# A table of relative biases fetched in two parts behind different weight units, and a small row fetched later

## The chip, the core and the metric

The kernel runs on one core of one Trainium2 chip. Its time is in device microseconds (us), from the start of one execution to its end, and the figure compared is the median of several executions. Inside the core five engines run side by side, each with an instruction stream of its own: TensorE (PE in the profile), VectorE (DVE), ScalarE (ACT), GpSimd (POOL) and SyncE (SP). They meet only at semaphores. SP, ACT and POOL also issue DMA transfers; each has a queue of its own (q1, q10 and q0 in the profile), and the queues share the core's 16 DMA engines.

## What is computed

Three transformer-like layers over one sequence of 256 tokens with 1024 channels, all in float32. Layer 0 attends with a relative position bias for each of eight heads, layer 1 is a differential attention with a scalar made from `diff_lambda`, and layer 2 is a convolution module. The change touches the inputs of the first two. Cut to what matters:

```python
def t5_bucket(rel): ...                       # distance -> one of 32 buckets
# layer 0: attention, for every head
rel_own = q_pos[:, None] - k_pos_own[None, :]
bias_own = jnp.moveaxis(rel_table[t5_bucket(rel_own)], -1, 0)
s_own = einsum('bhqd,bhkd->bhqk', qb, k_own) + bias_own[None]
s_own = jnp.where(rel_own >= 0, s_own, NEG_INF)
p = jax.nn.softmax(...)
# layer 1: differential attention
lam_full = (jnp.exp(jnp.sum(lam32[0] * lam32[1])) - jnp.exp(jnp.sum(lam32[2] * lam32[3]))
            + lambda_init)
a = p[:, :, 0] - lam_full * p[:, :, 1]
```

## The kernel before

The program has six stages, `s` = 0 to 5: attention, gated product, attention, gated product, convolution, gated product. Weights arrive in *units* of 128 x 1024 float32 (512 KB). A unit goes into one of eight slots of `raw`; ACT rounds it into `whi` (L893), DVE writes the rest into `wlo` (L1203), and PE multiplies both with the two parts of the activations (`h_hi`, `h_lo`). Semaphore `ld[u]` says that slot `u` has landed, `hi[u]` and `lo[u]` that it has been split. The helper `prep(u, n)` on ACT and on DVE is one half of this split.

In stage 0 the order is as follows.

- SP first loads 16 quarters of `ada_w` for the modulation vectors (L305), which DVE sums into `acc` (L1225, L1228). Then it loads the units of the first pair of heads in the order of slots 0, 2, 1, 3, 5, 4 (L266): q and k of head 0, q and k of head 1, then the two halves of v. The next units (slot 0, slot 2 and so on for heads 2 and 3) follow as slots come free. A column unit is fetched in rows of 512 bytes.
- ACT issues the small parameters at the start (`params`, L909). The last of them is the lambda row: 256 floats repeated over 128 partitions into `lam_in`, which is a part of `mix` that is first read in stage 2.
- The bias is made in three steps. PE looks up a row of 384 values for each head, DVE adds the causal fill into `relrow` (L1282), and POOL stores it to a small tensor in memory, `rel_small` (L456). Then POOL reads it back skewed, so that partition p starts at element p + 1, into `head_bias` (L461): 128 partitions x 8 heads x 384. It does so in two transfers for all heads (columns 0 to 255, and 256 to 383), after waiting for `ld[3]`, the fourth unit. The two post-norm gain rows, `Ga` and `Gf` (L419), follow on the same queue.
- DVE waits for both bias transfers before the first head. The first DVE instruction that reads them is L1350, which adds the bias to a head's scores. The next ones find the row maximum (L1357, L1360), ACT takes the exponential (L1039), and DVE divides (L1365, L1369).

One attention step (`step`, head n) on ACT is, in this order: copy q (L1021), copy k (L1023), `prep` of two units for a later head (L893, twice), exponential (L1039), `prep` of one unit, copy v (L1048) on even heads, `prep` of one more unit, then q of the next head (L1021). On DVE: bias and maximum, two `prep`, division, more `prep` and some steps of the modulation sums (L1215), which read quarters of `ada_raw`. PE does q and k of a head (L491), the scores (L662, L663), v (L686) on even heads, then q and k of the next head, and only then transposes this head's probabilities (L637), for which it also waits until ACT has copied the next q.

The `lam_in` row is used by `lam_and_gain` at the start of the second attention.

Of the kernel before, what the change touches and what calls it, by code (L numbers as in the profile page):

```python
# [61 lines left out]
def build(nc, x, c, rel_bias, ada_w, ada_b, norm_g, moba_w_qkv, moba_w_o, diff_w_qkv, diff_w_o,  # L62
# [4 lines left out]
    with ExitStack() as ctx:  # L67
# [114 lines left out]
        used = [sem(f"unit_multiplied{u}") for u in range(8)]  # L182
        ada_ld = [sem(f"ada_loaded{k}") for k in range(4)]
        odd_ld = [sem(f"first_odd_loaded{k}") for k in range(4)]
        gemv, first_mm, bias0_loaded = sem("gemv_steps"), sem("first_quarters_multiplied"), sem("first_bias_loaded")
        acc_zero, acc_bias = sem("acc_zero"), [sem(f"acc_bias{n}") for n in range(1, 7)]
        c_loaded, par_loaded, x_loaded = sem("c_loaded"), sem("par_loaded"), sem("x_loaded")
        rel_loaded, rel_mm, rel_row = sem("rel_loaded"), sem("rel_mm"), sem("rel_row")
        rel_stored, bias_loaded = sem("rel_stored"), sem("bias_loaded")
        lam_loaded, lam_seq, lam_exp = sem("lam_loaded"), sem("lam_seq"), sem("lam_exp")  # L190
        b2_loaded, gain_loaded = sem("b2_loaded"), sem("gain_loaded")
        id_zero, consts = sem("id_zero"), sem("consts")
# [208 lines left out]
        def _(pool):  # L401
# [38 lines left out]
            for s in range(LAST + 1):  # L440
                for t in range(TT):
                    pool.wait_ge(ssx_done, 2 * s + t + 1)
                    pool.tensor_tensor(rsx[:, t:t + 1], ssx[:, t:t + 1], mhalf, ALU.pow).then_inc(rsx_done, 1)
                if s in (2, 4):
                    pool.wait_ge(mod_gf, s // 2)
                    pool.wait_ge(hlo, h_parts_before(s + 1))
                    acc_init(s + 2, s // 2, 5 * D, 6 * D)
                    gains(s // 2)
                elif s in (1, 3):
                    pool.wait_ge(mod_ga, s // 2 + 1)  # L450
                    pool.wait_ge(mod_cols, s + 1)
                    pool.wait_ge(hlo, h_parts_before(s + 1))
                    acc_init(s + 2, s // 2 + 1, 0, 5 * D)
                if s == 0:
                    pool.wait_ge(rel_row, 1)
                    pool.dma_start(rel_small, relrow).then_inc(rel_stored, 16)  # L456
                    pool.wait_ge(rel_stored, 16)
                    pool.wait_ge(ld[3], 16)
                    for lo_c, hi_c in ((0, 2 * P), (2 * P, 3 * P)):
                        src = bass.AP(rel_small.tensor, rel_small.offset + 1, [[1, P], [REL, H], [1, hi_c - lo_c]])  # L460
                        pool.dma_start(head_bias[:, :, lo_c:hi_c], src).then_inc(bias_loaded, 16)  # L461
                    gains(0)
                if s == 2:
                    def head_rstd(i):
                        for at in range(2 * TT):
                            t = at % TT
                            pool.wait_ge(oss, i * 4 + at + 1)
                            pool.tensor_tensor(mso[:, t:t + 1], sso[:, t:t + 1], eps2, ALU.add).then_inc(oms, 1)
                            pool.wait_ge(oms, i * 4 + at + 1)
                            pool.tensor_tensor(rso[:, t:t + 1], mso[:, t:t + 1], mhalf, ALU.pow)\  # L470
                                .then_inc(ors, 1)
                    with pool.Fori(0, NI_A) as i:
                        head_rstd(i)
                if s == 4:
                    pool.wait_ge(lms_done, 1)
                    pool.tensor_tensor(ln_rs, ln_ms, mhalf.broadcast_to([P, TT]), ALU.pow).then_inc(lrs_done, 1)
                for t in range(TT):
                    rstd_y(s, t)
# [409 lines left out]
        def _(act):  # L888
# [44 lines left out]
            params(prow[2 * FT:4 * FT, 3, :], rows(f_dw_b_2), par_loaded)  # L933
            params(prow[0:16 * KT, 4, :], rows(a_dw_w_2[0, 0:16]), par_loaded)
            params(prow[0:15 * KT, 5, :], rows(a_dw_w_2[0, 16:CONV]), par_loaded)
            params(lam_in, bass.AP(diff_lambda.tensor, diff_lambda.offset, [[0, P], [1, 256]]), lam_loaded)

            pre_stats(0)
            for t in range(TT):
# [259 lines left out]
        def _(dve):  # L1199
# [120 lines left out]
            def attention(s):  # L1320
# [63 lines left out]
                def first_attention_step(i, j):  # L1384
                    n = i * 2 + j
                    last = n == H - 1

                    def sums(m0, m1):
                        for m in range(m0, m1):
                            gemv_step(0, FIRST + m // KT, m % KT)  # L1390

                    def between():

                        if n:
                            out_lo((n - 1) // 2, 1 - j)
                        if not last:
                            prep(j, i + (nb + 1))
                            prep(2 + j, i + (nb + 1))

                    m0, m1 = 2 * HEAD_QUARTERS[n], 2 * HEAD_QUARTERS[n + 1]  # L1400
                    ahead = m0 + (m1 - m0) // 2 if n > 1 else m0
                    sums(m0, ahead)
                    softmax(n + hb, n, None, between)
                    prep(6 + j, i + nb3)
                    if not last:
                        sums(ahead, m1)
                        prep(4 + j, i + (nb + 1))
# [308 lines left out]
            for s in range(LAST + 1):  # L1716
# [10 lines left out]
                        prep(4 + j, USE[s][2])  # L1727
                if s in (0, 2):
                    if s == 0:
                        dve.wait_ge(bias_loaded, 32)  # L1730
                        gemv_start(2)
                    else:
                        lam_and_gain()
# [51 lines left out]
```

## Time and profile before

| | |
|---|---|
| median of 3 executions | 1019.33 us (1019.18 to 1020.24) |
| the profiled execution's own time | 1019.02 us |
| its span, from the first to the last instruction | 1017.2 us |
| PE busy | 975.5 us (96%) |
| DVE busy | 844.4 us (83%) |
| ACT busy | 543.9 us (53%) |
| moved by DMA | 233.52 MB, mean 230 GB/s |
| mean granted TensorE clock | 0.978 of full |

PE is the engine that is seldom idle; all others have slack on average. Averages hide that stage 0 begins with the transfers at their limit, so the first 60 us have to be read by themselves. In the rows further down, a number in brackets at the end of a row is the idle time of the engine before that row, and behind the arrow stands what ended it.

### The profile page before, as it was taken

Reading aid. Unit: us, or ns where it says so; the run is one execution under the profiler, and the core shown is the slowest. Engines: PE = TensorE matmul, PEld = TensorE weight load, DVE = VectorE, ACT = ScalarE, POOL = GpSimd, SP = SyncE. Lnnn points to the kernel's source line nnn. Section 1 sums busy time; section 2 is a strip of 40 time slices with the busy share of each in tenths; the row PEclk is TensorE's granted clock in tenths of the full one; section 3 lists DMA queues with packets and bytes.
Section 4 is the critical chain, followed back from the end, with each engine's and each line's share of the span. In section 5 each row is a group of like instructions: output and inputs, shape, how many; then the busy total and the mean of one; then the engine's idle time right before and its main releaser. Section 6 shows DMA issues by size and latency. Waiting matters only on the chain.

```text
span 1017.2 us, 19351 instructions
## 1 busy us (share of the span) xinstructions
PE 975.5 (96%) x6742; PEld 892.6 (88%) x6742; DVE 844.4 (83%) x1381; ACT 543.9 (53%) x1016; POOL 57.7 (6%) x99
## 2 busy tenths in 40 slices
PE   5899999999999999998999999999998999999997
PEld 4889988999999888996999999979995889999996
DVE  5869988888888779777898888889998879997775
ACT  2455545454444467555544444459997455555552
POOL 2100002000000012112200000010000000000000
PEclk9999998999999999999999999999998989999999
DMA  9999982999999865661699999974330548966641
GB/s 338 325 333 317 318 272 77 348 340 337 309 312 310 259 187 165 168 196 54 182 347 340 330 311 310 302 232 126 105 103 21 153 125 239 269 186 186 186 124 42
DMA packets 259087, 233.52 MB, mean 230 GB/s; under 512 B 7513, under 2 KB 208986, under 8 KB 259034
## 3 DMA queue, kind: packets, MB, share of 16 engines
q1 hardware_dynamic: 256256, 226.52, 73.2%
q0 software_dynamic: 1504, 4.80, 1.3%
q10 hardware_dynamic: 1274, 1.52, 0.4%
q8 instruction: 30, 0.49, 0.2%
q14 instruction: 23, 0.19, 0.1%
HBM read 231.75 MB, written 1.06 MB: 229 GB/s over the span
## 4 chain that ended last, share of the span: by engine, by line
PE 49%; DVE 8%; issue 4%; ACT 2%; POOL 1%; DVEq 0%; POOLq 0%; ACTq 0%
PE work L491 29%; PE Y L511 14%; DVE mix L1645 3%; PE work L686 2%; ACT whi L893 1%; DVE wlo L1203 1%; DVE xt L1317 1%; DVE acc L1215 1%; PE Y L848 0%; DVE Y L1313 0%; ACT h_hi L964 0%; PE Y L803 0%; POOL small L427 0%; PE work L652 0%; PE work L668 0%
## 5 line engine op out<-in xcount | busy, mean ns | idle before, releaser
L491 PE MATMUL work<-h_hi,whi 128*128 128x256 f32 x1440 | 409.0, 284 | 7.3 <-DVE h_lo L1261 5.9
L1203 DVE TENSOR_TENSOR wlo<-raw,whi 128x1024 fp32r<-128x1024 f32 x286 | 347.1, 1222 | 77.3 <-ACT whi L893 77.0
L491 PE MATMUL work<-h_hi,wlo 128*128 128x256 f32 x1440 | 403.9, 280 | 0.0
L491 PE MATMUL work<-h_lo,whi 128*128 128x256 f32 x1440 | 403.8, 280 | 0.0
L893 ACT ACTIVATE whi<-raw 128x1024 fp32r<-128x1024 f32 x286 | 298.0, 1054 | 150.0 <-PE work L491 44.0
L491 PEld LDWEIGHTS work<-h_hi,whi 128*128 128x128 f32 x1440 | 272.2, 189 | 15.8 <-DVE h_lo L1261 6.8
L491 PEld LDWEIGHTS work<-h_lo,whi 128*128 128x128 f32 x1440 | 272.0, 189 | 3.1
L491 PEld LDWEIGHTS work<-h_hi,wlo 128*128 128x128 f32 x1440 | 272.6, 189 | 0.0
L1215 DVE SCALAR_TENSOR_TENSOR acc<-ada_raw,csil,acc 128x512 f32<-128x512 f32 (+1 forms) x256 | 190.8, 747 | 6.0 <-DMA ada_raw<-in_ada_w 3.4
L511 PE MATMUL Y<-whi,ab_hi 128*128 128x512 f32 x308 | 97.7, 398 | 0.0
L511 PE MATMUL Y<-whi,ab_lo 128*128 128x512 f32 x308 | 96.7, 395 | 0.0
L511 PE MATMUL Y<-wlo,ab_hi 128*128 128x512 f32 x308 | 96.5, 394 | 0.0
L511 PEld LDWEIGHTS Y<-whi,ab_lo 128*128 128x128 f32 x308 | 57.7, 187 | 13.9
L511 PEld LDWEIGHTS Y<-wlo,ab_hi 128*128 128x128 f32 x308 | 57.8, 188 | 13.9
L511 PEld LDWEIGHTS Y<-whi,ab_hi 128*128 128x128 f32 x308 | 52.5, 188 | 7.0
L1645 DVE SCALAR_TENSOR_TENSOR mix<-mix,taps 128x256 f32<-128x256 f32 x128 | 51.4, 477 | 0.0
L1097 ACT ACTIVATE ab_hi<-mix 128x256 fp32r<-128x256 f32 x66 | 27.2, 412 | 39.1 <-DVE mix L1556 20.7
L427 POOL TENSOR_TENSOR small<-small 128x1 f32<-128x1 f32 x12 | 6.6, 554 | 703.2 <-DVE small L1311 703.2
L1089 ACT ACTIVATE mix<-work 128x256 f32<-128x256 f32 x44 | 16.7, 380 | 47.1 <-PE work L491 47.1
L1137 ACT ACTIVATE wlo<-ident,taps 128x128 fp32r<-128x128 f32 x104 | 40.4, 389 | 0.0
L1137 ACT ACTIVATE whi<-ident,taps 128x128 fp32r<-128x128 f32 x104 | 40.4, 389 | 0.0
L1039 ACT ACTIVATE mix<-mix,small 128x128 f32<-128x128 f32 (+1 forms) x48 | 21.4, 447 | 34.5 <-DVE small L1360 34.5
(206 smaller groups left out, 1180.3 us busy)
## 6 DMA issues: line engine op xcount, KB each, us to landing
ada_raw<-in_ada_w SPq DMA_DIRECT2D x88, 512.0 KB, 6.6
raw<-in_ffn_w_in SPq DMA_DIRECT2D x88, 512.0 KB, 7.8
ada_raw<-in_mod_w SPq DMA_DIRECT2D x48, 512.0 KB, 6.6
raw<-in_ffn_w_out SPq DMA_DIRECT2D x44, 512.0 KB, 5.7
raw<-in_f_up_w SPq DMA_DIRECT2D x44, 512.0 KB, 3.9
raw<-in_moba_w_qkv SPq DMA_DIRECT2D x24, 512.0 KB, 8.2
raw<-in_diff_w_qkv SPq DMA_DIRECT2D x24, 512.0 KB, 7.2
raw<-in_a_pw_w SPq DMA_DIRECT2D x24, 512.0 KB, 5.7
```

Source lines behind the costliest of these rows:

```text
L491: mm = pe.matmul(dst, w[:, u, ws], h[:, k, :], start=(k == 0 and m == 0), stop=(k == KT - 1 and m == 2))
L511: mm = pe.matmul(Y[:, 2 * t + f, :], a[:, ts], w[:, u, f * 512:(f + 1) * 512], start=(first and m == 0), stop=False)
L686: mm = pe.matmul(work[:, 1, t * S:(t + 1) * S], h[:, k, ts], w[:, 4:6, ws], start=(k == 0 and m == 0), stop=(k == KT - 1 and m == 2))
L893: act.activation(whi[:, u, :], raw[:, u, :], ACT.Copy).then_inc(hi[u], 1)
L1039: act.activation(pr[:, g, a:b], pr[:, g, a:b], ACT.Exp, bias=mneg[:, m:m + 1], accum_out=msum[:, m:m + 1]).then_inc(ex_done, 1)
L1089: act.activation(gate[:, j, :], work[:, 2 * j, 0:S], ACT.Silu).then_inc(gate_done, 1)
L1097: act.activation(a_hi[:, j, :], act32[:, j, :], ACT.Copy).then_inc(ahi, 1)
L1137: d = act.activation(diag[w][:, m, :], ident[:], ACT.Copy, scale=taps[:, j, 36 + w * NP + m:37 + w * NP + m])
L1203: dve.tensor_tensor(wlo[:, u, :], raw[:, u, :], whi[:, u, :].bitcast(F32), ALU.subtract).then_inc(lo[u], 1)
L1215: dve.scalar_tensor_tensor(at, ada_raw[:, k, q % 2, :], csil[:, ccol:ccol + 1], at, ALU.mult, ALU.add).then_inc(gemv, 1)
L1317: dve.scalar_tensor_tensor(xt[:, t, :], yG, rsy[:, t:t + 1], xt[:, t, :], ALU.mult, ALU.add).then_inc(x_ready, 1)
L1645: v = dve.scalar_tensor_tensor(sums, u[:, m:m + S], w, sums, ALU.mult, ALU.add)
```

## The change

`head_bias` is fetched in four transfers in place of two. The two column parts of head 0 are issued when `ld[0]`, the first unit, has landed; those of heads 1 to 7 when `ld[3]` has landed. There are two semaphores, and DVE waits for head 0's in front of head 0's L1350 and for the others' in front of head 1's. The lambda row is no longer ACT's last parameter but POOL's last transfer of this group, behind the gain rows. The numbers of bytes are the same.

```diff
-        rel_stored, bias_loaded = sem("rel_stored"), sem("bias_loaded")
+        rel_stored, bias_loaded = sem("rel_stored"), (sem("first_bias_loaded"), sem("other_biases_loaded"))
@@ POOL, stage 0
                     pool.wait_ge(rel_stored, 16)
-                    pool.wait_ge(ld[3], 16)
-                    for lo_c, hi_c in ((0, 2 * P), (2 * P, 3 * P)):
-                        src = bass.AP(rel_small.tensor, rel_small.offset + 1, [[1, P], [REL, H], [1, hi_c - lo_c]])
-                        pool.dma_start(head_bias[:, :, lo_c:hi_c], src).then_inc(bias_loaded, 16)
+                    for h0, h1 in ((0, 1), (1, H)):
+                        pool.wait_ge(ld[3 if h0 else 0], 16)
+                        for lo_c, hi_c in ((0, 2 * P), (2 * P, 3 * P)):
+                            src = bass.AP(rel_small.tensor, rel_small.offset + h0 * REL + 1,
+                                          [[1, P], [REL, h1 - h0], [1, hi_c - lo_c]])
+                            pool.dma_start(head_bias[:, h0:h1, lo_c:hi_c], src).then_inc(bias_loaded[h0], 16)
                     gains(0)
+                    lam_src = bass.AP(diff_lambda.tensor, diff_lambda.offset, [[0, P], [1, 256]])
+                    pool.dma_start(lam_in, lam_src).then_inc(lam_loaded, 16)
@@ ACT, the parameters
-            params(lam_in, bass.AP(diff_lambda.tensor, diff_lambda.offset, [[0, P], [1, 256]]), lam_loaded)
@@ DVE, first_attention_step
                     sums(m0, ahead)
+                    if n < 2:
+                        dve.wait_ge(bias_loaded[n], 32)
                     softmax(n + hb, n, None, between)
@@ DVE, between pre_norm and attention of stage 0
-                        dve.wait_ge(bias_loaded, 32)
                         gemv_start(2)
```

On POOL in stage 0, from the store of the bias rows to the first reciprocal root of the post-norm, the kernel before has these rows (names in brackets are the semaphores that a row waits for; `unit_loaded3` is `ld[3]`):

```order
L443 TENSOR_TENSOR small<-small 128x1 [waits ssx_done]
L456 DMA rel_small<-mix 8x384 [waits rel_row]
L461 DMA head_bias<-rel_small 128x8x256 [waits unit_loaded3,rel_stored]
L461 DMA head_bias<-rel_small 128x8x128
L419 DMA Ga<-in_norm_g 128x1024
L419 DMA Gf<-in_norm_g 128x1024
L427 TENSOR_TENSOR small<-small 128x1 [waits msy_done] x2
```

The changed kernel has, at the same place (its lines are numbered by its own text):

```order
L443 TENSOR_TENSOR small<-small 128x1 [waits ssx_done]
L456 DMA rel_small<-mix 8x384 [waits rel_row]
L463 DMA head_bias<-rel_small 128x256 [waits unit_loaded0,rel_stored]
L463 DMA head_bias<-rel_small 128x128
L463 DMA head_bias<-rel_small 128x7x256 [waits unit_loaded3]
L463 DMA head_bias<-rel_small 128x7x128
L419 DMA Ga<-in_norm_g 128x1024
L419 DMA Gf<-in_norm_g 128x1024
L466 DMA mix<-in_diff_lambda 128x256
L427 TENSOR_TENSOR small<-small 128x1 [waits msy_done] x2
```

Two small transfers have come ahead of the wait for the fourth unit, the two large ones have lost a head, and the lambda row stands last.

On ACT, at the end of the parameters and ahead of the squares of x, the kernel before has:

```order
L909 DMA mix<-in_f_dw_b 44x128
L909 DMA mix<-in_a_dw_w 128x128
L909 DMA mix<-in_a_dw_w 120x128
L909 DMA mix<-in_diff_lambda 128x256
L904 ACTIVATE xs,small<-xt 128x1025 x2
L941 ACTIVATE xs<-xt,small 128x1024 x2
```

and the changed kernel has:

```order
L913 DMA mix<-in_f_dw_b 44x128
L913 DMA mix<-in_a_dw_w 128x128
L913 DMA mix<-in_a_dw_w 120x128
L908 ACTIVATE xs,small<-xt 128x1025 x2
L944 ACTIVATE xs<-xt,small 128x1024 x2
```

Only the lambda row has gone; the rest keeps its order. DVE and PE keep the order of all their instructions.

## Rows read from the trace of the kernel before

**Rows 1.** The page: busy engines, and the DMA engines' busy share in 40 slices.

```profile
PE 975.5 (96%) x6742; PEld 892.6 (88%) x6742; DVE 844.4 (83%) x1381; ACT 543.9 (53%) x1016; POOL 57.7 (6%) x99
...
DMA  9999982999999865661699999974330548966641
```

**Rows 2.** Timeline of PE: start, us, line, idle before.

```profile
32.45 1.86 PE L589 MATMUL Y<-ones,acc 128*128 128x1 f32 x8 [1.37 <-DVE acc L1228]
36.27 0.55 PE L491 MATMUL work<-h_hi,whi 128*128 128x256 f32 x1 [1.96 <-DVE h_lo L1261]
...
46.30 0.36 PE L686 MATMUL work<-whi,h_hi 128*128 128x256 f32 x1
...
58.98 0.52 PE L637 MATMUL work<-ident,mix 128*128 128x128 f32 x3 [1.14 <-ACT mix L1021]
```

**Rows 3.** Timeline of DVE around the first head.

```profile
27.57 4.82 DVE L1228 SCALAR_TENSOR_TENSOR acc<-raw,csil,acc 128x512 f32<-128x512 f32 x6 [0.23 <-DMA raw<-in_ada_w]
...
40.39 5.76 DVE L1203 TENSOR_TENSOR wlo<-raw,whi 128x1024 fp32r<-128x1024 f32 x5
48.84 0.56 DVE L1350 SCALAR_TENSOR_TENSOR mix<-work,head_bias 128x384 f32<-128x384 f32 x1 [2.69 <-DMA head_bias<-rel_small]
...
50.16 1.22 DVE L1203 TENSOR_TENSOR wlo<-raw,whi 128x1024 fp32r<-128x1024 f32 x1
53.92 1.22 DVE L1203 TENSOR_TENSOR wlo<-raw,whi 128x1024 fp32r<-128x1024 f32 x1 [2.55 <-ACT whi L893]
```

**Rows 4.** Timeline of ACT, from its last parameter to the second head's q.

```profile
10.72 0.42 ACTq L909 DMA_DIRECT2D mix<-in_diff_lambda  x1
...
32.14 1.06 ACT L893 ACTIVATE whi<-raw 128x1024 fp32r<-128x1024 f32 x1 [11.32 <-DMA raw<-in_moba_w_qkv]
...
45.07 1.05 ACT L893 ACTIVATE whi<-raw 128x1024 fp32r<-128x1024 f32 x1
52.83 1.06 ACT L893 ACTIVATE whi<-raw 128x1024 fp32r<-128x1024 f32 x1 [6.71 <-DMA raw<-in_moba_w_qkv]
53.91 1.28 ACT L1039 ACT_TABLE_LOAD   x1
...
58.47 0.36 ACT L1021 ACTIVATE mix<-work 128x256 f32<-128x256 f32 x1
```

**Rows 5.** Timeline of POOL: the bias transfers and the last gain row.

```profile
38.10 1.84 POOL L461 DMA_DIRECT2D head_bias<-rel_small  x2 [15.83 <-DMA raw<-in_moba_w_qkv]
...
40.48 0.55 POOL L419 DMA_DIRECT2D Gf<-in_norm_g  x1
```

**Rows 6.** Stretches: length, busy us by engine, granted clock, DMA share, GB/s.

```profile
12.00:20.00 8.00, 6.56 (x27) 5.18 (x28) 5.60 (x9) 3.52 (x6) 1.14 (x2) 1.00 1.07 369
...
30.00:40.00 10.00, 6.63 (x28) 6.15 (x28) 8.26 (x16) 6.23 (x11) 1.90 (x3) 1.00 1.20 291
...
42.00:50.00 8.00, 7.38 (x59) 6.80 (x58) 5.28 (x7) 3.14 (x5) 0.00 (x0) 1.00 1.02 342
```

**Rows 7.** DMA queues in 42 to 50 us: packets, MB, share of 16 engines.

```profile
q0 software_dynamic: 638, 2.37, 85.7%
q1 hardware_dynamic: 698, 0.36, 15.8%
```

**Rows 8.** DMA issues in 0 to 75 us: KB each, median us to landing.

```profile
head_bias<-rel_small POOLq DMA_DIRECT2D x1, 1024.0 KB, 8.5
head_bias<-rel_small POOLq DMA_DIRECT2D x1, 512.0 KB, 9.8
...
mix<-in_diff_lambda ACTq DMA_DIRECT2D x1, 128.0 KB, 8.3
...
rel_small<-mix POOLq DMA_DIRECT2D x1, 12.0 KB, 4.8
```

**Rows 9.** Timeline of DVE, later in the same attention.

```profile
98.46 3.18 DVE L1215 SCALAR_TENSOR_TENSOR acc<-ada_raw,csil,acc 128x512 f32<-128x512 f32 x4 [1.05 <-DMA ada_raw<-in_ada_w]
```

**Rows 10.** Timeline of PE, at the end of the same attention.

```profile
142.72 0.55 PE L637 MATMUL work<-ident,mix 128*128 128x128 f32 x3 [0.28 <-DVE mix L1369]
```

More of the change, by code:

```diff
@@ L184, in build @@
         odd_ld = [sem(f"first_odd_loaded{k}") for k in range(4)]
-        gemv, first_mm, bias0_loaded = sem("gemv_steps"), sem("first_quarters_multiplied"), sem("first_bias_loaded")
+        gemv, first_mm, bias0_loaded = sem("gemv_steps"), sem("first_quarters_multiplied"), sem("mod_bias_loaded")
         acc_zero, acc_bias = sem("acc_zero"), [sem(f"acc_bias{n}") for n in range(1, 7)]
```

## The prediction

> **What bounds the kernel now.** I began with the page. PE is busy 96% of the span, and the DMA engines are at 9 tenths in each of the first six slices of 25 us [rows 1]. So two things can be late in stage 0: PE itself, or a transfer that PE's work hangs on. The next view is the timeline of PE, read for idle time only. From the first product on units at 36.27 us to the end of that attention PE stands still noticeably at three places: it starts only at 36.27, it waits 1.14 us at 58.98, and 0.28 us at 142.72 [rows 2, 10]. Between 58.98 and 142.72 no row of PE shows idle time. So whatever the change does in the first 60 us has to move one of these places.
>
> Who ends each? The start at 36.27 hangs on `h_lo`, which needs the modulation sums; DVE ends them at 27.57 + 4.82 = 32.39, and PE adds them up at 32.45 [rows 2, 3]. The first unit lands just as late, at 32.14 [rows 4].
>
> The wait at 58.98 was ended by ACT's copy of the next q (L1021) [rows 2]. On ACT's timeline the reader is to see that this copy, at 58.47, is the end of a chain without a pause: a `whi` at 52.83, the table load at 53.91, the exponentials, more `prep` and the v copy. And the `whi` at 52.83 had waited 6.71 us for a unit [rows 4]. ACT's program has two `prep` behind the k copy, slot 0 and slot 2; the rows at 45.07 and 52.83 are these. So the unit in slot 2 for heads 2 and 3, landing at 52.8, releases PE at 58.98.
>
> Beside it stands the wait that the change is about. DVE's L1350 began at 48.84, after 2.69 us of waiting for `head_bias` [rows 3]. It is real, but it isn't on the chain just read. DVE has the maximum ready about 1.3 us later (the next `wlo` starts at 50.16), and ACT comes to the exponential only behind the table load, at 53.91 + 1.28 = 55.19 [rows 3, 4]. That leaves 5.0 us of slack. DVE then waits again, 2.55 us at 53.92, for the same late unit [rows 3].
>
> **Part 1: DVE's wait for head 0.** Head 0's part is issued at `ld[0]`. ACT saw that at 32.14 [rows 4]. Two issues cost at most 1.84 us in all, by the large ones in [rows 5], so they are out by 34.0. Landing takes between 4.8 us (the 12 KB store) and 9.8 us (the longest of the two bias transfers) [rows 8]. So head 0's bias lands between 37 and 43.8. DVE is busy with five `prep` until 40.39 + 5.76 = 46.15 [rows 3], so in either case the wait goes. L1350 starts near 46.2 and the whole 2.65 us are removed. What is late next: `wlo` of slot 0 runs from about 47.5 to 48.7 and not 50.16 to 51.4, and then DVE stands before the same unit that lands at 52.8. Its wait there grows from 2.55 to about 5.2 us. Effect on the end: 0, with ACT's wait for slot 2 as the cover. If that cover were gone, it would be 2.65 us.
>
> **Part 2: when slot 2's unit lands.** This is what decides. From 12 us on the DMA engines are never below full share: 369 GB/s in 12 to 20, 291 in 30 to 40, 342 in 42 to 50 [rows 6]. With the queues always full, a unit lands when all bytes placed before it have gone through, so I count bytes.
>
> Head 0's part is 128 x 384 x 4 = 0.197 MB. It leaves the stretch at 42 to 50, where it is worth 0.197 / 342 GB/s = 0.57 us, and enters at about 34, where it costs 0.57 to, at 291 GB/s, 0.68 us. Both places are ahead of slot 2's unit. Net: 0 to +0.1.
>
> The lambda row is 128 x 1 KB = 0.131 MB. It was issued at 10.72 and landed 8.3 us later, at 19 [rows 4, 8], at 369 GB/s: 0.36 us. Now it is POOL's last transfer, issued near 40.48 + 0.55 = 41.0 [rows 5], at 342 GB/s: 0.38 us. POOL's queue is served strongly. In 42 to 50 it moved 2.37 MB in 638 packets (3.7 KB each), the units' queue 0.36 MB in 698 (0.5 KB each) [rows 7]. So I count the lambda row as ahead of slot 2's unit too. Net: 0.
>
> Beyond that the heads 1 to 7 stay where they were, behind `ld[3]` at 38.10 [rows 5]. That landing moves by -0.36 (lambda gone from in front) and +0.57 to +0.68 (head 0 put in front), about +0.3. POOL's later queue holds 0.131 - 0.197 = -0.066 MB, 0.2 us less. The two nearly cancel. Sum for slot 2's unit: 0 to +0.1 us, and I take +0.1.
>
> **Part 3: the start.** With 0.131 MB less ahead of them, the last quarters of `ada_w` and the first unit land up to 0.36 us sooner. DVE waited 0.23 us for such a quarter at 27.57 [rows 3]. PE could start at about 35.9, not 36.27. ACT also loses an issue of 0.42 us [rows 4]; its next work feeds transposes that come 10 us later. But this gain ends at 58.98: PE reaches the wait sooner and waits 1.14 + 0.36 = 1.5 us. Effect on the end: 0.
>
> Head 0's bytes delay the units of slots 1, 3, 5 and 4 by 0.3 us net. ACT and DVE take the last of them within the five `prep` that end at 46.15 [rows 3], and PE begins v at 46.30 [rows 2]. If that moved by 0.3 us it would again be taken back at 58.98.
>
> **Part 4: later.** Even if slot 2's unit came early, PE's gain would have to pass 142.72, where DVE ends its wait [rows 10]. DVE is behind a quarter that landed at 98.46 [rows 9], and nothing in the change makes that quarter land sooner, since the bytes in front of it are the same. The lambda row is first read in stage 2, long after it has landed. The added waits and transfers are on DVE and POOL, and none is on PE.
>
> **Sum.** The profiled execution took 1019.02 us, 0.3 below the median of the others. 1019.02 + 0 (part 1) + 0.1 (part 2) + 0 (parts 3 and 4) = 1019.1, and on the scale of the median 1019.33 + 0.1 = 1019.4.
>
> **Rule and row.** In 42 to 50 us the two queues were served nearly packet for packet, 638 to 698, and the larger packets took 87% of the bytes [rows 7]. The Trainium skill, page "DMA: Bandwidth & Descriptors", section on queues, rings and completion order, says that each DMA engine goes round its queue rows and drains a whole packet from one before it turns to the next. By that rule, and the trace agrees, a POOL transfer issued behind the first unit overtakes the units still queued on SP's row. It speaks against issuing head 0's part so early: it would put 0.57 us in front of the second unit.
>
> **The rivals.**
>
> *The bias wait was on the path (4%).* Then 2.65 us come off: 1016.7. For it speaks only that DVE waits. Against it are the 5.0 us of slack above.
>
> *Slot 2's unit lands sooner (14%).* If the DMA engines do not pass bytes on as evenly as I count, and head 0's 0.57 us and the start's 0.36 us both reach that unit, it lands 0.93 us sooner; the PE wait of 1.14 us could shrink by that. Time: 1018.4 to 1019.1. It needs the lambda row to go behind the unit, and 142.72 not to take it back.
>
> *Slower: POOL's transfers hold slot 2's unit longer (12%).* The place is 41 to 53 us. If the lambda row stands in front of the unit (+0.38) while the time that it frees at the start is lost in SP's issue order, and the seven-head transfers run at 291 GB/s and not 342 (their 1.376 MB then take 0.70 us more), the unit lands 1.1 us later. PE waits 2.2 us at 58.98, and the time is 1020.4. It decides when the unit lands after 53.2. To be told from no change it would have to land after 54.8.
>
> *Head 0's bytes delay the second unit (4%).* If they came in front of it, its `whi` would be late by up to 0.57 us and PE's start with it. By itself that is taken back at 58.98: 1019.3. It adds to the slower case only.
>
> *The clock (4%).* The mean granted clock is 0.978 (table above), so small shifts may move where it falls. I can't give it a sign; up to 2 us either way.
>
> My own case, within 0.3 us of before, has the remaining 62%.
>
> **How the numbers follow.** About 0.2% (2 us) is what a measurement of this kernel can tell from no change. The range takes in the gain of 0.93 us and the loss of 1.1 us: 1018.4 to 1020.4. Outside it stand the first rival and part of the clock's. Faster by more than 0.2%: 4% + 2% = 6%. Slower by more: 2% from the third rival, 2% from the clock, 4%. Same: 90%.
>
> **What would show it.** Right: L1350 of head 0 starts near 46.2 without a wait for `head_bias`; ACT's second `whi` behind the k copy still waits until 52.6 to 53.1; PE starts near 35.9 and its idle time before L637 grows to about 1.5 us. Wrong: that `whi` starts before 52.3 or after 53.3, or PE reaches 142.7 by over 0.5 us sooner or later. The prediction fails if some wait that I took as covered was the one that ended last, or if the DMA engines had gaps that the moved bytes now fill or open.

## The result, and the profile after

| | before | changed |
|---|---|---|
| median, alternating executions on one chip | 1019.2 us (11 runs, 1018.31 to 1020.32) | 1021.07 us (11 runs, 1019.97 to 1022.63) |
| ratio to the kernel before | | 1.0021, 95% interval 1.0013 to 1.0028 |
| profiled execution, own time | 1019.02 us | 1020.06 us |
| span | 1017.2 us | 1018.2 us |

The changed kernel is slower, by 0.21% as the ratio has it; the two medians lie 1.9 us apart. The prediction, 1019.4 us and no measurable change, was wrong. I first read what answers to [rows 1]: the page of the changed kernel.

```profile
PE 973.4 (96%) x6742; PEld 890.5 (87%) x6742; DVE 844.3 (83%) x1381; ACT 544.3 (53%) x1016; POOL 59.5 (6%) x102
```

The totals tell nothing: busy times have moved by 2.1 us at most, and POOL has its three instructions more. The mean granted clock of the whole span is 0.982 in this trace and was 0.978, so over the whole span the slower kernel had the faster clock. So the timelines are read again at the places that the prediction named. Line numbers of the changed kernel are 3 or 4 higher. DVE around the first head, as in [rows 3]:

```profile
45.61 0.56 DVE L1353 SCALAR_TENSOR_TENSOR mix<-work,head_bias 128x384 f32<-128x384 f32 x1
...
52.82 1.23 DVE L1206 TENSOR_TENSOR wlo<-raw,whi 128x1024 fp32r<-128x1024 f32 x1 [5.80 <-ACT whi L897]
54.59 1.23 DVE L1206 TENSOR_TENSOR wlo<-raw,whi 128x1024 fp32r<-128x1024 f32 x1 [0.55 <-ACT whi L897]
```

The wait of 2.69 us for `head_bias` is gone, and the next instruction on a unit waits 5.80 us instead. ACT, as in [rows 4], says why:

```profile
31.45 1.06 ACT L897 ACTIVATE whi<-raw 128x1024 fp32r<-128x1024 f32 x1 [10.99 <-DMA raw<-in_moba_w_qkv]
33.27 1.06 ACT L897 ACTIVATE whi<-raw 128x1024 fp32r<-128x1024 f32 x1 [0.76 <-DMA raw<-in_moba_w_qkv]
...
41.83 2.01 ACT L897 ACTIVATE whi<-raw 128x1024 fp32r<-128x1024 f32 x2 [0.85 <-DMA raw<-in_moba_w_qkv]
...
51.73 1.06 ACT L897 ACTIVATE whi<-raw 128x1024 fp32r<-128x1024 f32 x1 [7.22 <-DMA raw<-in_moba_w_qkv]
53.50 1.06 ACT L897 ACTIVATE whi<-raw 128x1024 fp32r<-128x1024 f32 x1 [0.71 <-DMA raw<-in_moba_w_qkv]
```

Three things are to be seen. The first unit is there 0.69 us sooner (31.45 for 32.14), as foreseen. Slot 2's unit is taken up 0.67 us later (53.50 for 52.83). And two waits are new: 0.85 us at 41.83 for a unit of the first group, and 7.22 us at 51.73 for slot 0's next unit, which before was there by 45.07 without a wait. Now the slot 2 unit comes right behind it.

Did SP ask for that unit later, or did it travel longer? SP's own rows say it. An issue row has its start and its length, a row of the issues has KB and the time from the issue's start to landing. The unit of slot 0 for heads 2 and 3, in the kernel before:

```profile
35.57 1.66 SPq L266 DMA_DIRECT2D raw<-in_moba_w_qkv  x1
raw<-in_moba_w_qkv SPq DMA_DIRECT2D x1, 512.0 KB, 8.1
```

and in the changed kernel:

```profile
34.94 3.27 SPq L266 DMA_DIRECT2D raw<-in_moba_w_qkv  x1
raw<-in_moba_w_qkv SPq DMA_DIRECT2D x1, 512.0 KB, 16.8
```

It was issued 0.63 us sooner and landed 16.8 us after the start of its issue and not 8.1 (34.94 + 16.8 = 51.7, where ACT takes it). Slot 2's unit was issued at 41.01 and before at 41.68, so 0.67 us sooner too, and took 12.5 us for 11.1. Nothing was asked for later; both units travelled longer.

PE, as in [rows 2, 10]:

```profile
35.60 0.55 PE L495 MATMUL work<-h_hi,whi 128*128 128x256 f32 x1 [1.95 <-DVE h_lo L1264]
...
59.65 0.52 PE L641 MATMUL work<-ident,mix 128*128 128x128 f32 x3 [2.88 <-ACT mix L1024]
...
143.97 0.49 PE L641 MATMUL work<-ident,mix 128*128 128x128 f32 x3
```

PE starts 0.67 us sooner and restarts 0.67 us later, so it stands still for 2.88 us and not 1.14 (it runs out of work at 56.77, before at 57.84). At the end of the attention it is 1.25 us late (143.97 for 142.72). The profiled execution as a whole took 1.04 us longer, so its loss is all there by the end of the first attention. The other 0.8 us between the medians lies in executions that have no trace here.

Last, the stretches: length, busy us by engine, granted clock, DMA share, GB/s.

```profile
36.00:38.00 2.00, 1.96 (x9) 1.67 (x9) 1.75 (x5) 1.72 (x4) 1.01 (x2) 1.00 0.99 224
...
59.00:66.00 7.00, 6.35 (x39) 6.06 (x40) 5.70 (x12) 6.19 (x13) 0.00 (x0) 0.76 1.11 322
```

The same two stretches of the kernel before:

```profile
36.00:38.00 2.00, 1.70 (x6) 1.43 (x6) 2.00 (x6) 1.54 (x4) 0.00 (x0) 1.00 1.19 292
...
59.00:66.00 7.00, 7.00 (x57) 6.68 (x58) 5.90 (x12) 5.80 (x12) 0.00 (x0) 1.00 1.14 322
```

In 36 to 38 us the DMA engines move 224 GB/s where they moved 292, and their busy share falls from 1.19 to 0.99. In 59 to 66 us the granted clock averages 0.76 of full: for a part of that stretch it is at the lower level, 1.2 GHz, right after PE's standstill.

That made three suspects: the place of head 0's transfers, the place of the lambda row, and the clock.

### The profile page after: what moved, and what is told of

It reads as the page before. It is cut to its first block, busy times and chain, and to the rows that moved or that the text cites. A ratio compares the mean times of both kernels' runs of the same rounds, so it can differ in the third digit from the quotient of the medians.

```text
span 1018.2 us, 19353 instructions
## 1 busy us (share of the span) xinstructions
PE 973.4 (96%) x6742; PEld 890.5 (87%) x6742; DVE 844.3 (83%) x1381; ACT 544.3 (53%) x1016; POOL 59.5 (6%) x102
## 3 DMA queue, kind: packets, MB, share of 16 engines
HBM read 231.75 MB, written 1.06 MB: 229 GB/s over the span
## 4 chain that ended last, share of the span: by engine, by line
PE 37%; DVE 8%; issue 4%; ACT 2%; POOL 0%; DVEq 0%; POOLq 0%; ACTq 0%
PE work L495 24%; PE Y L515 12%; DVE mix L1650 4%; ACT whi L897 1%; DVE wlo L1206 1%; DVE acc L1218 1%; ACT h_hi L967 1%; DVE xt L1320 1%; PE Y L852 0%; DVE Y L1316 0%; DVE ab_lo L1635 0%; POOL small L427 0%; DVE h_lo L1264 0%; DVE mix L1645 0%; DVE xs L1657 0%
## 5 line engine op out<-in xcount | busy, mean ns | idle before, releaser
L690 PE MATMUL work<-whi,h_hi 128*128 128x256 f32 x128 | 36.0, 281 | 0.9 <-DVE mix L1338 0.7
```

What stands on the lines that cost most here:

```text
L690: mm = pe.matmul(work[:, 1, t * S:(t + 1) * S], h[:, k, ts], w[:, 4:6, ws], start=(k == 0 and m == 0), stop=(k == KT - 1 and m == 2))
```

## The experiments

For each run I read the same places. "Slot 2" is the `whi` of that unit for heads 2 and 3, "from first" is its distance from the first unit's `whi`, "PE idle" the wait before the first head's transposes, "end" the start of the last head's first transposes (142.72 in [rows 10]). In s6 and s7 ACT takes slot 2's unit at another place of its order, so these fields are empty.

| run | median us | ratio [95%] | slot 2 | from first | PE idle | end | clock 59 to 66 | GB/s 36 to 38 |
|---|---|---|---|---|---|---|---|---|
| before | 1019.2 | | 52.83 | 20.69 | 1.14 | 142.72 | 1.00 | 292 |
| changed | 1021.07 | 1.0021 [1.0013, 1.0028] | 53.50 | 22.05 | 2.88 | 143.97 | 0.76 | 224 |
| s1 split only | 1021.10 | 1.0026 [1.0012, 1.0040] | 53.10 | 21.29 | 2.01 | 143.93 | 0.76 | 257 |
| s2 lambda only | 1019.79 | 1.0007 [0.9998, 1.0015] | 52.85 | 21.24 | 2.10 | 143.80 | 0.76 | 291 |
| s3 gap filled | 1019.77 | 1.0012 [1.0003, 1.0021] | 54.23 | 21.39 | none | 145.12 | 1.00 | 205 |
| s5 before, filled | 1020.12 | 1.0012 [1.0003, 1.0021] | 52.46 | 19.54 | none | 144.14 | 1.00 | 296 |
| s4 gains later | 1021.64 | 1.0031 [1.0019, 1.0043] | 50.67 | 18.89 | none | 144.77 | 1.00 | 204 |
| s6 exp first | 1020.23 | 1.0006 [0.9996, 1.0017] | | | 1.56 | 143.53 | 1.00 | 224 |
| s7 before, exp first | 1019.06 | 1.0001 [0.9992, 1.0010] | | | none | 143.10 | 1.00 | 287 |
| s8 split at fourth | 1019.71 | 1.0011 [1.0001, 1.0020] | 52.60 | 20.27 | 0.73 | 143.25 | 1.00 | 291 |
| s9 before, `Gf` late | 1017.76 | 0.9980 [0.9970, 0.9989] | 50.53 | 17.95 | none | 141.28 | 1.00 | 291 |
| s10 changed, `Gf` late | 1019.05 | 0.9998 [0.9989, 1.0007] | 52.06 | 20.01 | 0.88 | 141.85 | 1.00 | 214 |
| s11 before again | 1019.63, one run | | 52.69 | 20.44 | 1.30 | 142.28 | 1.00 | 298 |
| s12 changed again | 1019.92, one run | | 53.33 | 21.34 | 1.77 | 143.29 | 1.00 | 210 |

Ratios are to the kernel before in the same session. Its own median differed by up to 0.7 us between sessions (1018.92 to 1019.59), so a ratio below 1.001 is not told from none. The medians of two sessions are not subtracted here.

### s1 and s2: one part alone

s1 is the changed kernel with the lambda row back among ACT's parameters:

```diff
                     gains(0)
-                    lam_src = bass.AP(diff_lambda.tensor, diff_lambda.offset, [[0, P], [1, 256]])
-                    pool.dma_start(lam_in, lam_src).then_inc(lam_loaded, 16)
@@ ACT, the parameters
+            params(lam_in, bass.AP(diff_lambda.tensor, diff_lambda.offset, [[0, P], [1, 256]]), lam_loaded)
```

> The changed kernel with the lambda row back as ACT's last parameter, so the bias split alone. Late-unit theory (POOL's bytes and their packets hold the units for heads 2 and 3): the split alone moves the seven-head transfers ahead of the units in slots 5, 4 and 0 and keeps PE's idle time before the first L641 above 2 us; time 1020.3 to 1021.3. Lambda theory (the 0.13 MB behind the gain rows are what came in front of slot 2's unit, and the start that came 0.67 us sooner only lengthens the wait): the split alone is neutral, idle about 1.1 to 1.5 us, time 1019.0 to 1019.6.

s2 is the kernel before with only the lambda row moved:

```diff
                     gains(0)
+                    lam_src = bass.AP(diff_lambda.tensor, diff_lambda.offset, [[0, P], [1, 256]])
+                    pool.dma_start(lam_in, lam_src).then_inc(lam_loaded, 16)
@@ ACT, the parameters
-            params(lam_in, bass.AP(diff_lambda.tensor, diff_lambda.offset, [[0, P], [1, 256]]), lam_loaded)
```

> The kernel before with only the lambda row moved to POOL behind the gain rows. Late-unit theory: PE starts 0.4 to 0.7 us sooner, slot 2's unit lands within 0.4 us of before, PE's idle time before L637 is 1.5 to 2.0 us, time 1019.2 to 1019.8. Lambda theory: slot 2's unit lands 0.4 us or more later, idle above 2 us, and the time is that of the whole change, about 1021.

The split alone costs as much as the whole change (1.0026), the lambda row alone nothing that can be told (1.0007, interval across 1). ACT's timeline of s1 has both new waits, that of s2 neither. Of s1:

```profile
42.49 2.01 ACT L895 ACTIVATE whi<-raw 128x1024 fp32r<-128x1024 f32 x2 [1.18 <-DMA raw<-in_moba_w_qkv]
...
51.34 1.06 ACT L895 ACTIVATE whi<-raw 128x1024 fp32r<-128x1024 f32 x1 [6.29 <-DMA raw<-in_moba_w_qkv]
```

In s2 slot 2's unit is where it was (52.85 for 52.83) while PE starts 0.52 us sooner, at 35.75: the wait grows, the restart does not move. That is what the prediction had said of the lambda row. The split is what moves the unit: by 0.27 us in s1's trace, less than in the whole change. Slot 0's next unit took 16.1 us to land in s1 and 8.2 in s2.

But s2's trace shows something else as well. Its restart is where it was (59.00 for 58.98), its clock falls in 59 to 66 us, and its end comes at 143.80, 1.08 us late, with no wait of PE there. In s1 the restart is 0.26 us late and the end 1.21. So in both traces most of the loss at the end of the attention arose behind the restart.

### s3 and s5: the gap filled

Eleven products on constants keep PE going between the second head's k and the first head's transposes. s3 is the changed kernel, s5 the kernel before with the same lines.

```diff
+                    if s == 0 and n == 1:
+                        for _ in range(FILL):
+                            pe.matmul(Y[:, 0, 0:P], ident[:], ones[:], start=True, stop=True)
                     if n:
                         probs_T(T - 1)
```

> The changed kernel with 11 idle products (128x128 float32, about 2.4 us, into a bank that is overwritten later) in front of the first L641, where PE waited 2.88 us in the changed kernel. Nothing else is changed. Clock theory: the granted clock fell to half for 3.4 us at 61.0 us because PE had stood still, and that is most of the 1.9 us; with the gap filled there is no fall near 61 us and the time is 1019.3 to 1020.0. Late-unit theory alone (the time lost is just the unit's lateness): the fill changes nothing, 1020.8 to 1021.3.

> The kernel before with the same 11 idle products in front of the first L637. A control for the filled gap: in the kernel before PE waited 1.14 us there and the profile showed no fall of the clock near 60 us. If the fill cost or gave time by itself, it shows here. Clock theory: 2.4 us of products in a gap of 1.14 us put PE about 1.2 us later, so 1019.5 to 1020.5, the same as or slower than before. If the fill is a gain in itself (a clock that often falls in the kernel before too), 1018.0 to 1018.8.

With the gap filled the clock of the changed kernel stays at full in 59 to 66 us (1.00 in the table), and the median, 1019.77 us, is in the range expected if the clock were most of the loss. s5's, 1020.12, is in the range expected of its control. Both filled kernels stand at 1.0012. So with the same work in the gap the split shows no cost of its own, but the intervals reach from 1.0003 to 1.0021 and would hide 1 us. The point estimate of s3 is below that of the changed kernel (1.0012 against 1.0021), with intervals that overlap. This speaks for a part of the clock in the loss, and does not prove it. The profiled executions of s3 and s5 began their first unit 0.7 to 0.8 us later than before, so their absolute times are not compared; and s3's trace is of the slowest of its 12 executions (1022.75 us).

### s4: the gain rows later

```diff
+                    pool.wait_ge(ld[2], 32)
                     gains(0)
```

> The changed kernel, in which POOL waits for the second landing in slot 2 before it issues the gain rows and the lambda row (1.18 MB). If POOL's bytes hold the unit, it lands 2 us or more sooner (before 51.5 us), PE's idle time before L641 goes to under 0.5 us and the time falls below the kernel before: 1017.5 to 1019.0. If the unit is held by something else (its issue, the units in front of it), the landing and the time of the changed kernel stay, 1020.5 to 1021.5.

Here 1.18 MB (two gain rows of 0.52 MB, the lambda row of 0.13) leave the stretch before slot 2's unit. That unit comes at 50.67, and PE's standstill at the first transposes is gone. Yet it is the slowest run of all (1.0031), where 1017.5 to 1019.0 us had been expected of an early unit. DVE's timeline of s4 shows where the bytes went:

```profile
73.33 1.54 DVE L1219 SCALAR_TENSOR_TENSOR acc<-ada_raw,csil,acc 128x512 f32<-128x512 f32 x2 [4.08 <-DMA ada_raw<-in_ada_w]
75.66 1.54 DVE L1219 SCALAR_TENSOR_TENSOR acc<-ada_raw,csil,acc 128x512 f32<-128x512 f32 x2 [0.79 <-DMA ada_raw<-in_ada_w]
```

DVE now waits 4.87 us for quarters of `ada_w` where it waited 2.25 in the changed kernel and 2.35 in the one before, and at the end of the attention PE waits 0.51 us for DVE's probabilities at 144.77. The transfers put off inside a stretch in which the DMA engines never rest were not saved: they made the next ones late.

### s6 and s7: the exponential ahead of slot 2's unit

On ACT the first head's exponential is placed ahead of the `prep` of slot 2. s6 is the changed kernel, s7 the kernel before.

```diff
                         prep(j, i + (nb + 1))
-                        prep(2 + j, i + (nb + 1))
+                        if s or n:
+                            prep(2 + j, i + (nb + 1))
@@ behind the exponential
+                    if s == 0 and n == 0:
+                        prep(2, nb + 1)
```

> The changed kernel, in which ACT, for head 0 alone, takes the exponential before the split of slot 2's unit and not behind it. What follows the unit's landing on ACT shrinks by the table load and the exponentials, 2.3 us. If the wait of PE at the first L641 is this chain behind the unit, PE's idle time goes from 2.9 to 0.4 to 0.8 us, the clock does not fall at 61 us, and the time is 1018.0 to 1019.3. If PE is held by something else (the DVE sums behind their quarters), the idle time goes and the time stays within 0.5 us of the changed kernel.

> The kernel before with the same order on ACT. Here head 0's maximum is ready only at 50.2 us, still ahead of the unit at 52.8. By my theory the early bias is worth nothing even so: the idle time of 1.14 us goes, and the time is 1017.8 to 1019.0, equal to or below the same order in the changed kernel. If the earlier bias is worth its 2.65 us once the unit no longer stands before the exponential, the changed kernel with this order is faster than this one by 0.5 us or more.

This was to take away the cover under which the prediction had put the bias wait. The early bias would then let s6 beat s7. It doesn't: 1.0006 [0.9996, 1.0017] against 1.0001 [0.9992, 1.0010]. But the pair is no clean test. In s6 ACT waits 6.73 us for slot 0's unit, which lands at 51.73 as in the changed kernel, so the exponential is still held, by a unit, and PE's standstill is 1.56 us where 0.4 to 0.8 had been expected. Only in s7 is the cover gone: there ACT waits 1.34 us, until 49.70, for the row maximum behind DVE's late bias. What an early bias without a late unit would be worth, no run shows.

s7, which has no standstill of PE at all at the first transposes, isn't faster than the kernel before: PE then waits for DVE at 143.10 (0.48 us), and DVE had waited for a quarter of `ada_w` (3.88 us at 72.38). There are two paths to the end of the attention, and shortening PE's alone gave nothing here.

### s8: the same four transfers, all behind the fourth unit

```diff
                     for h0, h1 in ((0, 1), (1, H)):
-                        pool.wait_ge(ld[3 if h0 else 0], 16)
+                        pool.wait_ge(ld[3], 16)
```

(The lambda row is on ACT, as in s1.)

> Four bias transfers, but all behind the fourth unit, and the lambda row on ACT as before. It tells the early place of head 0's part from the cutting itself. If the early place is what makes the fourth unit seen sooner (36.99 to 37.4 us and not 38.1) and sends the large transfers ahead of the units in slots 5, 4 and 0, slot 2's unit lands at 52.5 to 52.9 here, PE's idle time is 1.0 to 1.5 us and the time 1018.8 to 1019.6. If the cutting (smaller transfers, one head apart) costs by itself, the landing is at 53.1 or later and the time over 1020.2.

Against s1 only the place of head 0's part differs. Slot 2's unit is back at 52.60, PE's standstill is 0.73 us, ACT's new waits are gone, slot 0's next unit lands 7.7 us after its issue (16.1 in s1), and 36 to 38 us reads as before (291 GB/s). Only later is there a dip:

```profile
42.00:44.00 2.00, 2.00 (x18) 2.00 (x19) 2.00 (x3) 1.99 (x3) 0.33 (x1) 1.00 0.76 267
```

So it is the early place and not the cutting into four that delays the units. DVE's L1352 begins at 46.47 and without a wait for `head_bias` here too: two small transfers ahead of the large ones were enough for that. The ratio is 1.0011 [1.0001, 1.0020], below the 1.0026 of s1 with intervals that overlap, and not clearly 1. DVE's wait for its quarter is longer here (3.76 us at 72.83), but whether the dip in 42 to 44 us (share 0.76) makes it so isn't shown: s7 has 3.88 us of that wait without such a dip.

### s9 and s10: bytes that leave the stretch for good

`Gf` and the lambda row are first needed after the first attention. Here they are issued one stage later. s9 is the kernel before with that, s10 the changed kernel.

```diff
-                for g, src in zip((Ga, Gf), post):
+                for g, src in list(zip((Ga, Gf), post))[:2 if layer else 1]:
@@ POOL, start of the second stage
+                    if s == 1:
+                        pool.dma_start(Gf[:], row(norm_g[0, 3])).then_inc(gain_loaded, 16)
+                        lam_src = bass.AP(diff_lambda.tensor, diff_lambda.offset, [[0, P], [1, 256]])
+                        pool.dma_start(lam_in, lam_src).then_inc(lam_loaded, 16)
```

> The kernel before with the second gain row and the lambda row (0.66 MB) fetched one stage later, when the DMA engines are at about a third of their share; bias and first gain row as before. If PE's wait of 1.1 us at the first L637 is set by the bytes ahead of slot 2's unit, the unit lands 1.5 us or more sooner, the idle time goes to under 0.5 us, the clock stays up at 60 us and the time is 1017.6 to 1018.7 (before 1019.0). If DVE's sums behind the ada quarters hold PE again at 142 us, the idle time goes and the time stays within 0.3 us of before.

> The changed kernel's bias split with the same late second gain row and late lambda row. The early bias of head 0 is worth nothing by my theory, since the unit still stands before the exponential on ACT: time equal to or up to 1 us above the other kernel of this pair, 1017.6 to 1019.5, and PE's idle time at the first L641 under 1.5 us, so that the clock stays up at 60 us. If the split costs by itself (units of slots 5, 4 and 0 held up), the idle time is above 1.5 us and the time 1019.5 to 1020.5.

s9 is faster than both kernels: 0.9980 [0.9970, 0.9989]. It keeps the two transfers for all heads, and DVE still waits 1.07 us for the bias. s10, the same with the split, is at 0.9998 [0.9989, 1.0007]; the two ran in one session. This is the cleanest price of the split: 0.9998 - 0.9980 = 0.18%, 1.8 us by the ratios and 1.3 us by the two medians, though the ends of the intervals just touch. It is more than the 1 us at most that had been expected, and PE's standstill in s10 is only 0.88 us. Slot 2's unit lands 20.01 us behind the first in s10 and 17.95 in s9. In neither trace does the clock fall in 59 to 66 us, so as far as the two traced executions go that fall is not what makes the difference.

### s11 and s12: both kernels once more, for a second trace

> The kernel before once more, unchanged, for a second profile. Clock theory: PE's idle time before the first L637 is again below 2 us (0.7 to 1.6) and the granted clock in 59 to 66 us is 1.00. If the clock falls there in the kernel before as well, its fall is no part of the difference.

> The changed kernel once more, unchanged, for a second profile. Clock theory: PE's idle time before the first L641 is again 2 us or more, slot 2's unit is taken up at 53.0 us or later, the third and fourth `whi` behind the columns wait for a unit (0.6 to 1.2 us at about 42 us), and the granted clock in 59 to 66 us is about 0.76. If the idle time is under 1.6 us here, the first profile was an exception and the cause of the 1.9 us is open.

The shift repeats: slot 2's unit at 53.33 against 52.69 (+0.64), PE's restart at 59.48 against 58.84 (+0.64), the end at 143.29 against 142.28 (+1.01). ACT has both new waits again. But PE's standstill is 1.77 us in s12, where 2 us or more had been expected, and the clock does not fall, where 0.76 had been:

```profile
59.00:66.00 7.00, 6.52 (x54) 6.23 (x55) 5.80 (x12) 6.30 (x14) 0.00 (x0) 1.00 1.10 322
```

So the fall is no fixed part of the changed kernel. Nor is the clock the same elsewhere in executions of one kernel: in 36 to 38 us it is at half in s11 (0.50) and at full in the first trace of the same kernel, and at half in s1, s3, s4 and s9 too.

## Why the prediction was wrong, point by point

**What bounds the kernel: right, but half of it.** (The sixth slice of the page is at 8 tenths and not at 9 as I wrote [rows 1]; nothing hangs on it.) Slot 2's unit does release PE's restart: in both pairs of traces the restart moved by exactly what the unit moved (+0.67 and +0.64 us). I had named 142.72 as a second bound and then treated it as one that only stops gains. It can also set the end when DVE's work is what is late: s3, s4, s6, s7, s8 and s9 each end in a wait of PE for DVE there (0.19 to 0.52 us). In the first trace of the changed kernel and in those of s1 and s2 PE does not wait there; its own path set the end, though DVE's quarter came at 72.22 for 71.65.

**Part 1, the bias wait: right.** L1353 starts at 45.61 without a wait; it could be sooner than the 46.2 foreseen since the whole program was 0.67 us sooner. The effect on the end was nothing. In every kernel with the early bias a late unit still stood before the exponential, so its worth without that cover stays untested.

**Part 2, slot 2's unit: this is the step that failed, a term that was counted at nothing.** "Head 0's part ... leaves the stretch at 42 to 50 ... and enters at about 34 ... Net: 0 to +0.1" and the sum "+0.1". Measured: +0.67 and +0.64, and from the first unit +1.36 (22.05 - 20.69) and +0.90 (21.34 - 20.44). The count of bytes was right as a count. What it supposed is that a unit lands when all bytes placed before it have gone through, and that they pass at the same rate in whatever order they come. Neither held. The rate first. In all seven traces with head 0's part early, 36 to 38 us moved 204 to 257 GB/s; in all seven others 287 to 298 (last column of the table). (292 - 224) GB/s over 2 us is 0.14 MB, at 342 GB/s 0.4 us. It is in part made up at once: 38 to 42 us passes 327 GB/s, before 306.

Then the order. The queues of the changed kernel in 32 to 53 us (packets, MB, share of 16 engines) show who paid:

```profile
q1 hardware_dynamic: 6848, 3.87, 68.6%
q0 software_dynamic: 784, 2.75, 40.3%
```

and those of the kernel before:

```profile
q1 hardware_dynamic: 7205, 4.07, 74.1%
q0 software_dynamic: 704, 2.62, 36.2%
```

POOL's queue moved 0.13 MB more, the lambda row, and the units' queue 0.20 MB less; at 342 GB/s that is 0.58 us of units, against 0.67 measured. This sum is only an estimate of the size: in s1, s2 and s8 the units' queue moved 3.98, 3.98 and 3.95 MB in that stretch, and slot 2's unit was there at 53.10, 52.85 and 52.60.

What tells the kernels apart is who was overtaken. POOL's large transfers went out 1.11 us sooner (36.99 for 38.10, and 37.47 for 38.20 in s12 and s11), where the prediction had them 0.3 us later. Since they are served as strongly as [rows 7] show, they overtook what the units' queue still held: the last two units of the first group, which in the kernel before had landed by then (the wait at 41.83), and slot 0's next unit, issued at 34.94. That unit took 13.3 to 16.8 us to land in all seven traces with head 0's part early, and 7.0 to 8.2 in all seven others. So ACT had to wait for it until 48.9 to 51.7 us, where in the kernel before it was there by 45.07, and slot 2's unit stood behind it in the same queue. Why the fourth unit, after which the large transfers go, came sooner and not later isn't known.

That the early place delays the units is shown, by s8 against s1; that the split costs time, by the changed kernel and s1. That it is the early place which costs the time is less firm: s8's interval overlaps that of s1, and those of s10 and s9 touch. Why the rate dips isn't known: head 0's two transfers are the smallest in the stretch, and s8 has such a dip as well, in both kernels 4 to 5 us behind their issue (163 GB/s in 37 to 38 us after 32.01, 157 in 42 to 43 after 38.24), but no run varied their size alone. And s8 shows that a dip alone doesn't cost the restart.

**Rule and row.** The Trainium skill, page "DMA: Bandwidth & Descriptors", section on queues, rings and completion order, has the DMA engines take whole packets from their queue rows in turn, and I weighed that it "would put 0.57 us in front of the second unit". The second unit was not late (33.27 - 31.45 = 1.82 us behind the first, before 1.81), as it had landed before POOL's bytes flowed. By that rule, and the trace agrees, POOL's transfers overtake what is still queued, and that was the fifth and sixth unit (the wait at 41.83) and slot 0's next. I applied it to the wrong unit.

**Part 3, the start: right, at twice the size.** PE started at 35.60, not 35.9: 0.67 us sooner and not 0.36. s2 started 0.52 and s1, with the lambda row left where it was, 0.32 us sooner, and s11 0.11 us later than the first trace of the same kernel (s12 stands 0.24 us before s11), so only some of it is the lambda row; the rest is within what one trace differs from the next. It was given back at the restart, as foreseen. What I left out is that the gift has a price: a standstill of 2.01 to 2.88 us (s1, s2, changed) lies where one of 1.14 was, and the clock fell behind it.

**The clock: a rival that I gave 4% and no sign.** In these traces it has a sign. The standstills of 2.01, 2.10 and 2.88 us (s1, s2, changed) were each followed by the lower level in 59 to 66 us, those of 1.77 us and less (s12, s6, s11, before, s10, s8) and the filled ones were not, nor were s4, s7 and s9, which have no such standstill. What it costs can be told only roughly. From the restart to the end the changed kernel took 143.97 - 59.65 = 84.32 us with the fall and, in s12, 143.29 - 59.48 = 83.81 without, 0.5 us. s2 with the fall took 84.80 and the kernel before 83.74 without, 1.06 us. But s8 took 84.50 with no fall, so not all of such a difference need be the clock.

**The sum.** In the first pair of traces the restart is +0.67 and what follows up to the end +0.58 (84.32 for 83.74), +1.25 together. In the second pair it is +0.64 and +0.37 (83.81 for 83.44), +1.01, with no fall of the clock in either. So the restart, the step that failed, is a little over half; the rest arises behind it, and how much of that the clock took in the first pair is not shown. The nearest rival was the third, "POOL's transfers hold slot 2's unit longer": it named the place, the direction and the limit after which it decides (53.2), and gave 1020.4. I gave it 12% since I needed three small losses to fall together for it. That it came near is in part luck: one of its terms was that the seven-head transfers run at 291 GB/s, and 38 to 42 us ran at 327.

**What stays open.** The medians differ by 1.9 us, the traced executions by 1.04 and, for s12 and s11, by 0.29. What the executions without a trace lose beyond these isn't seen. They may have the clock's fall more often or longer, but how often it falls in each kernel wasn't measured; s10 against s9, with no fall in either trace, speaks for a cost that is there without it.

## What to carry to other kernels

- A wait that the profile shows is not a gain to be had until the engine behind it has nothing else to wait for. Here the first head's exponential stood behind a late unit, which left 5 us of slack, and moving the bias only moved bytes ahead of that unit.
- While the DMA engines are full, a count of bytes can miss what a reordering costs (0 to 0.1 us counted, 0.67 measured). Look also at which queue is being overtaken, and read the rate of the stretch after the edit. Here a transfer in the queue with 3.7 KB packets went ahead of what was queued in packets of 0.5 KB [rows 7]. What helped was to take bytes out of the stretch altogether: s9 did that with 0.65 MB that nobody needed yet, and is the version to keep, 0.20% faster than the kernel before.
- If PE is made to start sooner but not to restart sooner, its standstill grows, and the clock may fall after it.

## What was unexpected of the hardware

- Two transfers of 64 and 128 KB put among full queues were followed by a stretch in which the DMA engines had gaps: busy share 0.93 to 1.02 in 36 to 38 us, with 1.19 before, and 204 to 257 GB/s for 292.
- With POOL's larger packets ahead, a unit of 512 KB in 512-byte rows took 13.3 to 16.8 us from issue to landing for 7.0 to 8.2, and SP's issue of it lasted 2.01 to 3.65 us for 1.57 to 1.68.
- Standstills of PE of 2.01, 2.10 and 2.88 us were followed by the lower level of the granted clock, and one of 1.77 us in the same place wasn't. The mean of 59 to 66 us was 0.76 in all three cases, whatever the length of the standstill.
